# A one-core encoder step: more down tiles in three passes, retrieval pairs moved ahead of them, and a PSUM read moved first

## The reference, cut to what matters

```
o = (att @ v) + (q @ S) * decay                        # retention, per head
o = o * rsqrt(mean(o * o, axis=-1) + EPS)              # group norm per head and token
y_ret = silu(rg) * o
...
s = einsum('thpd,pkd->thpk', q, sub_keys)              # product keys, top 16 per side, top 16 of the sums
g = softmax(ts)
a = gelu(einsum('thkd,td->thk', u_tab[e], hb))         # e: the 128 chosen experts of a token
out = einsum('thk,thkd->td', g * a, v_tab[e])
```

## Time and profile before

| | |
|---|---|
| median of 3 runs | 2280.32 us (2267.29 to 2287.32) |
| the profiled execution | 2273.49 us |
| its span | 2271.7 us |
| TensorE busy | 2210.6 us (97%) |
| VectorE busy | 1653.5 us (73%) |
| ScalarE busy | 538.2 us (24%) |
| GpSimd busy | 799.2 us (35%) |
| moved by DMA | 735.36 MB, mean 324 GB/s |

### The profile page before, as it was taken

The page is one execution under the profiler, slowest core; times in us unless marked ns, Lnnn a source line. Parts: engine busy times, 40 slices in busy tenths (PEclk is TensorE's granted clock), DMA queues, the critical chain, the costliest instruction groups (busy, mean ns, idle before and its releaser), DMA issues.

```text
span 2271.7 us, 30091 instructions
## 1 busy us (share of the span) xinstructions
PE 2210.6 (97%) x10245; PEld 1654.9 (73%) x10245; DVE 1653.5 (73%) x3164; ACT 538.2 (24%) x1083; POOL 799.2 (35%) x606
## 2 busy tenths in 40 slices
PE   6999989999999999999999999999999999999998
PEld 5988988999998975655565655677756666666664
DVE  3566575566665278989889989889847777777775
ACT  3212222122222111111211212233322222222221
POOL 4322221233333005574574665101124444344430
PEclk9999999999999999999999999999999999999999
DMA  4999898899972459999999999778889999999992
GB/s 160 309 303 330 274 315 295 301 312 311 323 258 109 158 188 372 338 410 412 371 412 413 390 412 412 273 252 276 265 330 413 413 395 394 387 391 392 399 399 82
DMA packets 326436, 735.36 MB, mean 324 GB/s; under 512 B 30368, under 2 KB 179616, under 8 KB 326304
## 3 DMA queue, kind: packets, MB, share of 16 engines
q1 hardware_dynamic: 202080, 439.67, 54.2%
q0 software_dynamic: 73728, 268.47, 30.2%
q10 hardware_dynamic: 50496, 25.59, 3.7%
HBM read 604.04 MB, written 129.57 MB: 323 GB/s over the span
## 4 chain that ended last, share of the span: by engine, by line
PE 87%; DVE 5%; DMA 4%; SPq 1%; issue 1%; POOL 1%; ACT 0%; another core or an unknown queue 0%; ACTq 0%; DVEq 0%; POOLq 0%
PE ps L1748 29%; PE ps L1809 12%; PE ps L1708 6%; PE ps L1512 5%; PE ps L1513 5%; PE ps L1514 5%; PE ps L1801 5%; PE ps L1803 5%; PE ps L1802 4%; DMA b<-in_u_t 4%; PE ps L1763 4%; DVE b L1030 1%; PE ps L1532 1%; SPq L480 1%; PE ps L1533 1%
## 5 line engine op out<-in xcount | busy, mean ns | idle before, releaser
L1748 PE MATMUL ps<-b,b 128*128 128x384 f32 x2048 | 669.0, 488 | 5.3 <-ACT b L882 3.7
L1748 PEld LDWEIGHTS ps<-b,b 128*128 128x128 f32 x2048 | 388.3, 191 | 270.6 <-issue 9.5
L677 POOL DMA_INDIRECT b<-u_rows,b x256 | 254.0, 992 | 797.5 <-DVE b L1374 600.5
L677 POOL DMA_INDIRECT b<-in_peer_v,b x256 | 336.7, 1315 | 116.5 <-DVE ps L1392 57.9
L1512 PE MATMUL ps<-b,b 128*128 128x320 f32 x1152 | 365.8, 318 | 1.6 <-issue 1.6
L642 POOL TENSOR_TENSOR b<-b,b 128x1024 fp32r<-128x1024 f32 x80 | 195.5, 2447 | 472.0 <-ACT b L690 467.5
L1513 PE MATMUL ps<-b,b 128*128 128x320 f32 x1152 | 358.1, 311 | 0.0
L1514 PE MATMUL ps<-b,b 128*128 128x320 f32 x1152 | 357.8, 311 | 0.0
L1392 DVE SCALAR_TENSOR_TENSOR ps<-b,b,ps 128x1024 f32<-128x1024 f32 x252 | 323.6, 1284 | 45.0 <-ACT b L898 29.6
L1374 DVE CUSTOM_DVE_ANT_0 b<-b,b 128x1024 f32<-128x1024 f32 x256 | 312.8, 1222 | 17.3 <-DMA b<-u_rows,b 12.3
L1030 DVE STREAM_TRANSPOSE b<-b 128x1024 f32<-128x1024 f32 x128 | 157.6, 1240 | 181.2 <-DMA b<-in_u_t 175.6
(11 more groups left out here) (165 smaller groups left out, 2524.3 us busy)
## 6 DMA issues: line engine op xcount, KB each, us to landing
b<-in_u_t SPq DMA_DIRECT2D x256, 512.0 KB, 5.6
u_rows<-b SPq DMA_DIRECT2D x512, 128.0 KB, 4.3
b<-in_peer_v SPq DMA_DIRECT2D x128, 512.0 KB
b<-in_w_in SPq DMA_DIRECT2D x72, 512.0 KB
b<-in_wq SPq DMA_DIRECT2D x48, 512.0 KB
acts<-b SPq DMA_DIRECT2D x128, 192.0 KB
gates<-b ACTq DMA_DIRECT2D x12, 2048.0 KB, 7.6
b<-gates SPq DMA_DIRECT2D x32, 768.0 KB
```

What stands on the lines that cost most here:

```text
L677: nc.gpsimd.indirect_dma_start(slots[n % SLOTS][:, :], None, u_rows if kind == "u" else v_rows, bass.IndirectOffsetOnAxis(ap=row_id[:, r_ ...
L1748: last = nc.tensor.matmul(ps[:, 2 + e % UP_BANKS, 0:TD], w[:, k * P:(k + 1) * P], h2[:, k, SD:T], start=(k == 0), stop=(k == KT - 1))
```

## The change

1. three(e) holds for five tiles of six rather than for three of five. That makes 104 three-pass tiles.
2. Eight pairs rather than six are done among the one-hot blocks, one behind every sixth block rather than every eighth, and five more behind the last block, ahead of weigh(0). NPAIR_U goes from 75 to 82. ScalarE's places for their gelus are every third up tile from 99 on, and then the up tiles 121 to 125.
3. outputs() copies the mean squares with EPS added out of PSUM as its first operation, into the first 640 elements of kw, and increments ms_used there. The Newton step reads the copy. It is one VectorE operation more per head.

```diff
+BESIDE_HOTS = 8
+BEFORE_DOWNS = 5
@@ pair_at
     if b >= NPAIR_R:
-        return GATE_AT + 2 + 4 * (b - NPAIR_R)
+        i = b - NPAIR_R
+        return GATE_AT + 3 * i if i < BESIDE_HOTS else GATE_ENDS - 2 + i - BESIDE_HOTS
@@
-NPAIR_U = NPAIR_R + 6
+NPAIR_U = NPAIR_R + BESIDE_HOTS + BEFORE_DOWNS
@@ three
-    return e < NKEY - GROUP and e % 5 in (0, 2, 4)
+    return e < NKEY - GROUP and e % 6 != 5
@@ outputs
                 dve.wait_ge(orms_ready, g + 1)
+                kept = kw[:, :, :].rearrange("p a b -> p (a b)")[:, 0:T]
+                then(nc.vector.tensor_scalar(kept.rearrange("p (a b) -> p a b", a=2), ps[:, 5:8:2, 0:HALF], EPS, None,
+                                             ALU.add), ms_used, g + 1)
                 r_, v_ = sq[1], sq[0]
-                rr, vv = (t.rearrange("p (a b) -> p a b", a=2) for t in (r_, v_))
                 line.then(nc.vector.reciprocal(r_, v_))
                 line.then(nc.vector.tensor_tensor(v_, r_, r_, ALU.mult))
-                then(nc.vector.scalar_tensor_tensor(vv, ps[:, 5:8:2, 0:HALF], EPS, vv, ALU.add, ALU.mult),
-                     ms_used, g + 1)
+                line.then(nc.vector.tensor_tensor(v_, kept, v_, ALU.mult))
                 between()
@@
-            R_PER = 2 * 5 + 1 + 3 + 2
+            R_PER = 2 * 5 + 2 + 3 + 2
@@ vector, ahead of the down tiles
             for blk_ in range(TD // BLK):
                 onehots(blk_)
-                if blk_ % 8 == 6:
+                if blk_ % 6 == 4:
                     next_pair()
+            for _ in range(BEFORE_DOWNS):
+                next_pair()
```

## The result

| | before | after |
|---|---|---|
| median | 2280.32 us (9 runs, 2267.29 to 2289.91) | 2260.26 us (9 runs, 2255.52 to 2272.80) |
| ratio | | 0.9921 (0.9891 to 0.9950) |
| the profiled execution | 2273.49 us | 2268.83 us |
| TensorE busy | 2210.6 us | 2180.1 us |

The change makes the kernel 0.8% faster, about 18 us (11 to 25 by the interval), where 42 were forecast.

What follows compares the result with a forecast made beforehand. TensorE, 87% of the chain, was taken as the bound. Terms of -30.7 - 14 + 0.3 + 2 gave -42.4 us, taking the median from 2280.3 to 2238 us; range 2216 to 2260.

Steps and rivals of the forecast that it cites:

- Three-pass tiles, -30.7: Down stage: 30 more three-pass tiles, each 1.02 us shorter than a plain one, take 30.7 us off TensorE.
- rivals 3 and 4: Down stage: VectorE waits for ScalarE's high half, 2250 us, chance 0.05; or for both copies, 2304 us, 0.05.
- Transfers in that stage, 0: Down stage: demand of 388 GB/s stays under 412, costing zero, up to +9 us if only 380 came.
- Rival 2: Down stage: gathers and SP's loads each get half of 412 GB/s, costing 19 us: 2257 us, chance 0.07.
- Eight pairs among the one-hots, +0.3: One-hot stage: the first pair makes TensorE wait 0.4 us once; cost +0.3 us (0 to 2).
- Five pairs behind them, +2: Ahead of the down stage: leftover gathers compete with the first tiles' loads, 0 to +10 us, taken as +2.
- Mean squares copied first, -14: Retention rounds: TensorE's 13.0 us wait for the banks and low clock go; 11 to 18.5 us, taken as 14.
- rival 1: Retention rounds: u_t loads pace VectorE, TensorE waits as long a step later, no gain: 2252 us, chance 0.10.
- does not move at all: Round two: if VectorE's way to the masked scores stays put, 3.2 us of the copy's gain come back.
- For three rounds: Retention rounds: the copy's gain over all three is put at 11 to 18.5 us.

Runs made afterwards that it cites:

- the run of the tiles alone: Before with only the rule for three passes changed (104 tiles), all 53 pairs left among the down tiles: 2257.27 us, ratio 0.9870.
- the last two runs of the table: After with 114 three-pass tiles, with two pairs behind the one-hot blocks, then with none: 2241.58 us (0.9801) and 2241.99 us (0.9816).
- e7: After with two pairs rather than five behind the one-hot blocks, still 104 three-pass tiles: 2246.51 us, ratio 0.9841.
- the light runs: Before, and before with only the mean squares copied first, each with u_t loads cut to 16 of 128 partitions: 2267.95 and 2264.02 us.
- the run with the transposes moved: After with the two u_t transposes of scores() moved behind the masked scores: 2259.95 us, ratio 0.9906.
- the copy alone: Before with only the edit of outputs() that copies the mean squares first: 2275.86 us, ratio 0.9975.

## Why the prediction was wrong

The forecast was -42.4 us; the ratio says -18 (-11 to -25), and the median of 2260.26 us lies just outside the range of 2216 to 2260. By stages, leaving out the retrieval part: -33.5 in the down stage, +18.2 ahead of it, -1.7 at the first query matmul (about -4 in the mean of the nine profiles that have the copy, which differ by 7 us among themselves), +0.4 in the one-hot stage. That makes -16.6.

**Three-pass tiles, -30.7: right,** 33.5 by the stage; a three-pass tile takes 4.10 us and not 4.13, which over 104 tiles is the difference. The groups of the down stage in after (busy us, mean ns, idle before), counterpart of the earlier trace rows, show the cover that was named, too:

```profile
L1437 DVE TENSOR_TENSOR b<-b,b 128x1024 fp32r<-128x1024 f32 x103 | 125.5, 1218 | 7.0 <-ACT b L948 6.3
...
L948 ACT ACTIVATE b<-b 128x1024 fp32r<-128x1024 f32 x103 | 108.0, 1048 | 63.4 <-PE ps L1809 45.1 <-DMA b<-in_peer_v 16.7 <-issue 1.5
...
L1430 DVE TENSOR_TENSOR b<-b,b 128x384 f32<-128x384 f32 x127 | 71.6, 565 | 83.1 <-PE ps L1809 69.6 <-PE ps L1815 12.6 <-issue 0.9
...
L1443 DVE TENSOR_TENSOR b<-b,b 128x384 fp32r<-128x384 f32 x104 | 57.1, 549 | 0.0
```

The operations cost what they cost before. VectorE waits 82 us for TensorE in place of 136 and is still ahead of it. L1437 waits for ScalarE's high half 6.3 us in 103 tiles, so rivals 3 and 4 did not come.

**Transfers in that stage, 0: right for this change.** The balance held, 395 GB/s and no idle TensorE, and the run of the tiles alone shows what it was worth: with 53 pairs the stage is 9 us longer than with 51 (the run with none behind the one-hots). That is the 4.2 MB of two pairs at 412 GB/s, 10 us: once the transfers are the bound, a pair costs its bytes. The same price separates the last two runs of the table, 11 us for two pairs. (The upper bound of this term was too low: 10.02 MB at 380 GB/s are 26.4 us a period, 12 us over the stage and not 9.) Rival 2, an even split of the rate between gathers and SP's loads, did not come in the stage.

**Eight pairs among the one-hots, +0.3: right.** From the first scatter to the last up matmul it is 231.3 us against 230.9, and no wait of TensorE there exceeds 0.7 us.

**Five pairs behind them, +2: this step failed,** by 16 us. Its own count was right: 10.5 MB of gathers, 5 MB of slack, 5.5 MB left over, which are 13 us at 412 GB/s. What failed is the choice of +2 out of 0 to +10, with the reason that SP's queue "isn't behind them in order, only beside them". Beside them is enough. The last store of gates shares the transfer engines with the gathers, and group_in(0) must wait for it in an in-order queue, with the stores of acts behind it and ScalarE's last eviction behind those. The claim that tile 0 is loaded from 1658 on is true but does not help, for a first product needs gates. The bound of +10 was too low, since it did not hold even the 13 us worked out beside it. That the pairs are the cause is shown: with none behind the blocks the start is back at 3.8 us.

How they act is less clear. One way is the order, the store starved by gathers and everything held by SP's queue. The other is the amount. The store was starved: 34.5 us, 8.7 with the gathers held, at most 12.4 in long rows. But both cures moved the start of the stage by 3.5 to 4.6 us out of 18 only. For the amount speaks the price of the last three pairs, 15.0 us measured and 15.3 by their bytes, and that the engines of after run full, at 390 to 419 GB/s in each stretch of 5 us from 1650 to 1690. The two pairs of e7 fit the count but for 3 us (4.2 of 5 MB). The order has a part at the end: from 1690 to 1695, while SP's queue waits and begins again, the engines move 142 GB/s, which gives away 3 us.

Neither cure tests the order by itself. Long rows for the store made small pieces for the loads; and holding the gathers left the engines half idle, since it held those of three early pairs. The trace of after shows gathers that could wait. Of all that GpSimd issues behind the store's issue at 1658.55, only the one at 1659.04 is for the five pairs. The 14 from 1660.28 to 1679.26, 7.3 MB, fill slots for pairs of the down stage, the first of which VectorE takes up at 1709.58. That is more than the 5.5 MB left over. No run held just these, so whether an order exists that saves the five pairs is open.

The Trainium skill's page DMA: Bandwidth & Descriptors (Queues, rings and completion order) has each engine take its queue rows in turn, a packet at a time. The store is in line with it: the page of the profile gives its queue 50496 packets of 507 bytes, 263 for each engine and store, and the gathers packets of 3641 bytes. If each of the store's had to let one of the gathers' pass, at 412 / 16 = 25.8 GB/s an engine would need 263 x 0.161 = 42 us. That is an estimate to set beside the 34.5, and it takes what the profile counts as a packet for one turn of an engine, which no run here shows. The rate falls behind 1690, so the gathers may have run out before the store ended.

**Mean squares copied first, -14: this step failed, and rival 1 was true in the main.** The banks' wait went, and the clock stayed up behind it: 16 transposes take 1.91 us in each round, where they took 3.65 in the earlier trace rows. But the gain was some 6 us at the w_out matmuls and about 4 at the first query matmul. Timelines of after, round one and round two:

```profile
222.78 0.67 DVE L1057 TENSOR_TENSOR b<-ps,b 128x128 f32<-128x128 f32 x2
...
223.50 6.19 PE L1637 MATMUL ps<-b,b 128*128 128x512 f32 x16 [3.89 <-DVE b L1057]
```

```profile
283.85 0.79 DVE L1098 TENSOR_SCALAR b<-ps 128x640 f32<-128x640 f32 x1
284.67 4.15 DVE L1101 RECIPROCAL b<-b 128x640 f32<-128x640 f32 x1
...
284.83 1.91 PE L1578 MATMUL ps<-b,b 128*128 128x128 f32 x16
...
315.61 0.67 DVE L1057 TENSOR_TENSOR b<-ps,b 128x128 f32<-128x128 f32 x2
316.33 4.21 PE L1637 MATMUL ps<-b,b 128*128 128x512 f32 x6 [3.18 <-DVE b L1057]
```

The copy takes the 0.79 us that it was priced at. The last masked scores of the second round come at 315.61; in the earlier trace rows they come at 315.33. VectorE has not moved at all, in the third round neither (408.84 against 409.13), and in the first it comes 1.2 us later (222.78 against 221.57). Its time is set by the loads of u_t; the light runs show it, as does the run with the transposes moved. What sets the pace of the loads themselves was not tested. The prediction had this very case, the way that "does not move at all" and gives 3.2 us back, and for round two it holds to a few tenths: the values' matmuls start 321.17 - 316.33 = 4.8 us earlier. The error is in "For three rounds". The 5.2 us of room is not there anew in each round: the values' matmuls start 2.1, 4.8 and 6.3 us earlier in the three, measured from the start of the program, and not by another 4 or 5 us each time. It is the one distance between TensorE and a VectorE that follows an outside clock, and once used up it is gone; so the three rounds together give what the last one has, some 6 us at most and not 11 to 18.5.

That the range's edge lay at the measured time is luck in part: rivals 1 and 2 had set it, rival 1 was nearly true, and the rest came from a cost that was in no rival.

Open: what makes the first query matmul profit less than w_out, 1.7 us against 5.8 in after (a wait for L1226, 2.3 us, in the w_out stage, which the other profiles lack), why the copy alone lengthens the query stage, and why the stretch with the retrieval differs by 16 us between executions.

## What to carry to other kernels

When a change moves transfers into a slack, count the bytes against the slack and book what is left over at the full rate, up to the first instruction that needs any byte of it; "in another queue" is no cover while the engines run full. When a stall is removed from a loop, ask whether the engine waited for follows its partner or an outside clock such as a stream of loads: in the second case the room is had once, not once an iteration. And when a wait changes its name and keeps its size, as it did in three of these runs, look first at what was full meanwhile: a cure by order is refuted only if nothing stood idle because of it.

## What the runs showed of the hardware

- A store of 2 MB in pieces of 512 bytes took 34.5 us beside gathers in rows of 4 KB, at most 10.9 us without them, and at most 12.4 us beside them when it was stored in rows of 16 KB.
- SP needed 8.10 us to issue one load of acts while a load in 512-byte pieces ran ahead of it (gates in long rows), against 0.43 us in after.
- One core's transfers reached 407 to 417 GB/s in the fullest stretches of 20 us, and 412 over 480 us, with different mixtures of gathers, loads and stores.
- Behind the idle time of 21.5 us TensorE ran at its lower level first: the granted clock is 0.50 from 1690 to 1705 and 1.00 from 1710 on; in the chain of after the first matmuls stand 0.43 us apart, and from 1708.40 on 0.23 us, 1.2 and then 2.4 GHz.
